# A two-group MoE encoder on one core: gate/up products of the next expert pair ahead of the down products of the current one

## The chip, the cores and the metric

The kernel runs on one core of a Trainium2 chip. The metric is the device time of one launch in microseconds (us). Everything is float32.

## What is computed

The reference is one step of a two-layer encoder over 576 tokens (512 of `x_prompt`, 64 of `x_sample`, width 1024). Layer 0 mixes tokens by banded attention, layer 1 by a convolution module; behind each comes the same kind of mixture of experts, which is what this change is about. Cut to that part:

```python
# N_GROUPS = 4, EXPERTS_PER_GROUP = 8, TOP_K_IN_GROUP = 2, D_MODEL = 1024, D_EXPERT = 256
g_w, g_idx = lax.top_k(g_probs, 1)               # one group per token
top_v, top_i = lax.top_k(in_group, TOP_K_IN_GROUP)   # two experts in it
...
hid = jax.nn.silu(jnp.einsum('nd,edf->nef', xt, w_gate[sl])) * jnp.einsum('nd,edf->nef', xt, w_up[sl])
hid = hid * gates[:, sl, None].astype(hid.dtype)
y = y + jnp.einsum('nef,efd->nd', hid, w_down[sl])
```

Each expert has 1 MB each of `w_gate`, `w_up` and `w_down`; a layer has 32 experts, 96 MB of weights.

## The kernel before

The kernel is written by hand for each engine: every engine runs a fixed list of instructions, and semaphores order them against each other. The stages follow one another: norm and attention, norm and router, experts of layer 0, gather and add; then norm and convolution, norm and router, experts of layer 1, gather and add; final norm.

**The expert stage.** The router gives each token two experts. Each expert has 64 slots (`CAP`), and two experts make a **pair** that fills 128 partitions; 16 pairs (`EPAIRS`) a layer. Tokens beyond 64 of one expert go to further (overflow) pairs, of which the data decide the number, at run time (`extra_turns`, `further`). For pair i (s = i % 2) the steps are:

- GpSimd gathers the pair's 128 rows of x from memory into `xe[s]` with one indirect DMA of 512 KB (L1095).
- *turn* (`ex_turn_pe`, L1168 to L1174): TensorE waits for these rows and transposes them in eight blocks into two PSUM banks (L1173). ScalarE copies one bank, VectorE the other, into `xte[s]` (`ex_turn_copy`, L1206).
- *gate/up* (`ex_up_pe`, L1176 to L1185): products of `xte[s]` with the pair's `w_gate` and `w_up` (L1183), into bank 2+s. ScalarE takes silu of one half into `sg` (L1211), VectorE multiplies it by the other half into `hid` (L1215).
- *down* (`ex_down_pe`, L1187 to L1202): TensorE transposes `hid` in two blocks (L1190), VectorE copies them into `hts` (L1219), TensorE waits for `w_down` and multiplies (L1200). ScalarE and VectorE each copy half of the result into `ysb[s]` (`ex_y_copy`, L1227).
- GpSimd scatters these 128 rows to memory with one indirect DMA of 512 KB (L1099).

`sg`, `hid` and `hts` exist once; `xe`, `xte`, `ysb` and the gate/up banks twice. Each engine runs its steps in the order in which `body` of `experts_pe`, `experts_act` and `experts_dve` names them, and a waiting instruction holds all that are behind it on its engine.

**Weights.** SyncE issues the loads (`experts_sync`). There are three buffers for gate/up (4 MB a pair, `GU_SLOTS`) and two for `w_down` (2 MB a pair). For pair i it waits until gate/up(i) is done, then issues the gate/up loads of pair i+3 (L1317), then waits until down(i) is done, and issues `w_down` of pair i+2 (L1321).

**GpSimd's list** (`experts_pool`): the gathers of pairs 0 and 1, some scatters for overflow rows, then for each i:

```python
if local + 2 < EPAIRS:
    pool.wait_ge(base.xt_mm, i + 1)      # turn(i) done
    rows_in(local + 2)                   # gather of pair i+2, L1095
...
pool.wait_ge(base.y_ev_a, i + 1 + FREE)  # both copies of y(i) done
pool.wait_ge(base.y_ev_d, i + 1 + FREE)
rows_out(local)                          # scatter of pair i, L1099
```

Behind the scatter of pair 14 it issues eight gathers (L1146) that bring finished result rows back to the tokens, then the scatter of pair 15, and, when that has landed and overflow pairs are done, the other gathers. The overflow pair, where there is one (here in layer 1), has its loads issued by SyncE when down(14) is done (L1366 to L1379).

Of the kernel before, what the change touches and what calls it, by code (L numbers as in the profile page):

```python
# [44 lines left out]
def encoder(nc, x_prompt, x_sample, cache_attn_k, cache_attn_v, cache_conv,  # L45
# [25 lines left out]
    EPAIRS = EXPERTS // 2  # L71
# [14 lines left out]
    with ExitStack() as ctx:  # L86
# [210 lines left out]
        base = ExpertSems("ex")  # L297
# [870 lines left out]
        def ex_turn_pe(pe, m, i, s, k):  # L1168
            pe.wait_ge(m.x_in[s], 16 * (k + 1))
            pe.wait_ge(m.xt_ev_a, i + FREE)  # L1170
            pe.wait_ge(m.xt_ev_d, i + FREE)
            for c in range(C):
                mm = nc.tensor.transpose(bank[c // 4][:, (c % 4) * P:(c % 4 + 1) * P], xe_pc[s][:, c, :], ident[:])  # L1173
            mm.then_inc(m.xt_mm, 1)  # L1174

        def ex_up_pe(pe, m, i, s, g, there):  # L1176
            pe.wait_ge(m.xt_ev_a, i + 1 + FREE)
            pe.wait_ge(m.xt_ev_d, i + 1 + FREE)
            pe.wait_ge(m.gu_in[g if m is base else 0], there)
            for c in range(C):  # L1180
                for e in range(2):
                    rr = slice(CAP * e, CAP * (e + 1))
                    mm = nc.tensor.matmul(bank[2 + s][rr, :], xte[s][:, c, rr], wgu[g][:, :, e, c, :],  # L1183
                                          start=c == 0, stop=c == C - 1)
            mm.then_inc(m.gu_mm, 1)  # L1185

        def ex_down_pe(pe, m, i, s, k, loads):  # L1187
            pe.wait_ge(m.hid, i + 1 + FREE)
            for c in range(FC):
                mm = nc.tensor.transpose(bank[4][:, c * P:(c + 1) * P], hid_pc[:, c, :], ident[:])  # L1190
            mm.then_inc(m.ht_mm, 1)
            pe.wait_ge(m.ht_ev, i + 1)
            pe.wait_ge(m.dn_in[s], 16 * loads * (k + 1))
            pe.wait_ge(m.y_ev_a, i + FREE)
            pe.wait_ge(m.y_ev_d, i + FREE)
            for h in range(2):
                for c in range(FC):
                    for e in range(2):
                        rr = slice(CAP * e, CAP * (e + 1))
                        mm = nc.tensor.matmul(bank[5 + h][rr, :], hts[:, c, rr], wdn[s][:, e, c, h * HALF:(h + 1) * HALF],  # L1200
                                              start=c == 0, stop=c == FC - 1)
            mm.then_inc(m.dn_mm, 1)  # L1202

        def ex_turn_copy(eng, copy, m, i, s, half, done):
            eng.wait_ge(m.xt_mm, i + 1)
            copy(xte[s][:, 4 * half:4 * half + 4, :], bank[half][:].rearrange("p (c r) -> p c r", c=4)).then_inc(done, 1)  # L1206

        def ex_silu_act(act, m, i, s):
            act.wait_ge(m.gu_mm, i + 1)
            act.wait_ge(m.hid, i + FREE)  # L1210
            nc.scalar.activation(sg, bank[2 + s][:, 0:FE], ACT.Silu).then_inc(m.silu, 1)  # L1211

        def ex_hid_dve(dve, m, i, s):
            dve.wait_ge(m.silu, i + 1)
            nc.vector.tensor_tensor(hid, sg, bank[2 + s][:, FE:2 * FE], ALU.mult).then_inc(m.hid, 1)  # L1215

        def ex_ht_dve(dve, m, i):
            dve.wait_ge(m.ht_mm, i + 1)
            nc.vector.tensor_copy(hts, bank[4][:, 0:FE].rearrange("p (c r) -> p c r", c=FC)).then_inc(m.ht_ev, 1)  # L1219

        def ex_y_copy(eng, copy, m, i, s, k, half, done):
            eng.wait_ge(m.dn_mm, i + 1)
            if m is base:
                eng.wait_ge(m.y_out[s], 16 * k + 16)
            else:
                eng.wait_ge(m.y_free, i + FREE)
            copy(ysb[s][:, half * HALF:(half + 1) * HALF], bank[5 + half][:]).then_inc(done, 1)  # L1227
# [4 lines left out]
        def gu_slot(l, local):  # L1232

            g = local % GU_SLOTS
            per_layer = len(range(g, EPAIRS, GU_SLOTS))
            return g, 32 * (per_layer * l + local // GU_SLOTS + 1)

        def turns(body, l):
            for local in range(EPAIRS):
                i = EPAIRS * l + local  # L1240
                body(i, i % 2, i // 2, local, local + 1 < EPAIRS)

        def extra_turns(eng, l, body):

            eng.wait_ge(further_known, 2 * l + 1)
            count = eng.value_load(over_count[0:1, 0:1], min_val=0, max_val=OPAIRS)
            with eng.If(count > 0):
                with eng.Fori(0, count) as it:
                    body(it)

        def experts_pe(pe, l):
            ex_turn_pe(pe, base, EPAIRS * l, 0, EPAIRS // 2 * l)

            def body(i, s, k, local, more):
                ex_up_pe(pe, base, i, s, *gu_slot(l, local))
                if more:
                    ex_turn_pe(pe, base, i + 1, (s + 1) % 2, k + (s + 1) // 2)
                ex_down_pe(pe, base, i, s, k, 1)

            turns(body, l)  # L1260

            extra = extras[l]

            def further(i):
                ex_turn_pe(pe, extra, i, 0, i)
                ex_up_pe(pe, extra, i, 0, GU_SLOTS - 1, 64 * (i + 1))
                ex_down_pe(pe, extra, i, 0, i, 2)

            extra_turns(pe, l, further)

        def experts_act(act, l):
            ex_turn_copy(act, nc.scalar.copy, base, EPAIRS * l, 0, 0, base.xt_ev_a)

            def body(i, s, k, local, more):
                ex_silu_act(act, base, i, s)
                if more:
                    ex_turn_copy(act, nc.scalar.copy, base, i + 1, (s + 1) % 2, 0, base.xt_ev_a)
                ex_y_copy(act, nc.scalar.copy, base, i, s, k, 0, base.y_ev_a)

            turns(body, l)  # L1280

            extra = extras[l]

            def further(i):
                ex_turn_copy(act, nc.scalar.copy, extra, i, 0, 0, extra.xt_ev_a)
                ex_silu_act(act, extra, i, 0)
                ex_y_copy(act, nc.scalar.copy, extra, i, 0, i, 0, extra.y_ev_a)

            extra_turns(act, l, further)

        def experts_dve(dve, l):
            ex_turn_copy(dve, nc.vector.tensor_copy, base, EPAIRS * l, 0, 1, base.xt_ev_d)

            def body(i, s, k, local, more):
                ex_hid_dve(dve, base, i, s)
                if more:
                    ex_turn_copy(dve, nc.vector.tensor_copy, base, i + 1, (s + 1) % 2, 1, base.xt_ev_d)
                ex_ht_dve(dve, base, i)
                ex_y_copy(dve, nc.vector.tensor_copy, base, i, s, k, 1, base.y_ev_d)

            turns(body, l)

            extra = extras[l]

            def further(i):
                ex_turn_copy(dve, nc.vector.tensor_copy, extra, i, 0, 1, extra.xt_ev_d)
                ex_hid_dve(dve, extra, i, 0)
                ex_ht_dve(dve, extra, i)
                ex_y_copy(dve, nc.vector.tensor_copy, extra, i, 0, i, 1, extra.y_ev_d)

            extra_turns(dve, l, further)
# [552 lines left out]
```

## Time and profile before

| | us |
|---|---|
| median of 3 runs (lowest, highest) | 1302.19 (1300.95, 1303.72) |
| the profiled execution, its own time | 1305.27 |
| its span in the trace | 1303.6 |
| TensorE busy in the span | 1067.0 (82%) |
| VectorE, ScalarE, GpSimd busy | 493.6, 289.5, 271.2 |
| granted TensorE clock, mean of the span | 0.91 |
| moved by DMA | 303.67 MB, mean 233 GB/s |

### The profile page before, as it was taken

Reading aid. Unit: us, or ns where it says so; the run is one execution under the profiler, and the core shown is the slowest. Engines: PE = TensorE matmul, PEld = TensorE weight load, DVE = VectorE, ACT = ScalarE, POOL = GpSimd, SP = SyncE. Lnnn points to the kernel's source line nnn. Section 1 sums busy time; section 2 is a strip of 40 time slices with the busy share of each in tenths; the row PEclk is TensorE's granted clock in tenths of the full one; section 3 lists DMA queues with packets and bytes.
Section 4 is the critical chain, followed back from the end, with each engine's and each line's share of the span. In section 5 each row is a group of like instructions: output and inputs, shape, how many; then the busy total and the mean of one; then the engine's idle time right before and its main releaser. Section 6 shows DMA issues by size and latency. Waiting matters only on the chain.

```text
span 1303.6 us, 14394 instructions
## 1 busy us (share of the span) xinstructions
PE 1067.0 (82%) x5242; PEld 617.5 (47%) x5242; DVE 493.6 (38%) x1066; ACT 289.5 (22%) x616; POOL 271.2 (21%) x289
## 2 busy tenths in 40 slices
PE   6999999996995897777762999987985987778780
PEld 5777777773453333333321777653543333333320
DVE  3234444443247111101116499994455111111116
ACT  3223232222111110000003355544111100000002
POOL 2000000000001221111033288860003110011033
PEclk9999999996996899888885899998995998888995
DMA  8953333212506899999955932100027999999764
GB/s 278 388 159 105 107 107 106 79 55 105 233 24 236 318 419 420 420 421 420 407 191 132 338 102 64 32 19 6 33 92 282 417 421 421 420 420 420 319 236 144
DMA packets 107791, 303.67 MB, mean 233 GB/s; under 512 B 18248, under 2 KB 65480, under 8 KB 82745
## 3 DMA queue, kind: packets, MB, share of 16 engines
q1 hardware_dynamic: 85481, 254.74, 50.5%
q0 software_dynamic: 22256, 48.22, 10.2%
q8 instruction: 33, 0.54, 0.2%
q14 instruction: 21, 0.17, 0.0%
HBM read 278.34 MB, written 57.12 MB: 257 GB/s over the span
## 4 chain that ended last, share of the span: by engine, by line
PE 66%; issue 16%; DVE 12%; ACT 2%; DMA 2%; POOL 1%; DVEq 0%; SPq 0%; another core or an unknown queue 0%; POOLq 0%
PE bank L1183 17%; PE bank L1200 11%; PE bank L522 10%; PE bank L421 8%; PE bank L549 4%; PE bank L1173 3%; DVE bank L1646 2%; PE bank L572 2%; PE bank L588 2%; PE bank L613 2%; PE bank L346 1%; PE bank L938 1%; DVE work L1219 1%; POOL ring L1146 1%; DVE work L1206 1%
## 5 line engine op out<-in xcount | busy, mean ns | idle before, releaser
L1200 PE MATMUL bank<-ring,work 128*64 128x512 f32 x528 | 149.9, 720 | 89.9 <-issue 80.4
L1183 PE MATMUL bank<-ring,work 128*64 128x512 f32 x704 | 158.9, 604 | 4.7 <-issue 3.8
L522 PE MATMUL bank<-arena,ring 128*128 128x288 f32 x512 | 131.9, 412 | 0.0
L1462 PE MATMUL bank<-arena,work 128*128 128x288 f32 x512 | 127.4, 410 | 5.1 <-DVE work L1627 2.6
L1200 PEld LDWEIGHTS bank<-ring,work 128*64 128x64 f32 x528 | 46.8, 165 | 170.1 <-issue 159.3
L421 PE MATMUL bank<-ring,arena 128*128 128x512 f32 x256 | 116.6, 611 | 7.4 <-ACT arena L1577 6.6
L1593 POOL TENSOR_TENSOR ring<-ring 128x606 f32<-128x606 f32 x76 | 103.8, 1366 | 57.0 <-ACT ring L1542 47.3
L1462 PEld LDWEIGHTS bank<-arena,work 128*128 128x128 f32 x512 | 97.6, 192 | 34.5 <-issue 4.0
L522 PEld LDWEIGHTS bank<-arena,ring 128*128 128x128 f32 x512 | 94.9, 190 | 32.6 <-issue 7.9
L1183 PEld LDWEIGHTS bank<-ring,work 128*64 128x64 f32 x704 | 56.2, 140 | 103.0 <-issue 101.7
L1215 DVE TENSOR_TENSOR work<-work,bank 128x256 f32<-128x256 f32 x33 | 13.9, 421 | 226.2 <-ACT work L1211 226.2
L1646 DVE SCALAR_TENSOR_TENSOR bank<-work,ring,bank 128x606 f32<-128x606 f32 x129 | 98.9, 846 | 0.0
L1183 PE MATMUL bank<-arena,work 128*64 128x512 f32 x352 | 79.3, 603 | 2.5 <-DVE work L1206 2.5
L1095 POOL DMA_INDIRECT work<-x_rows,tok_at x32 | 33.1, 1034 | 228.2 <-DVEq L1035 219.0
L421 PEld LDWEIGHTS bank<-ring,arena 128*128 128x128 f32 x256 | 49.0, 196 | 64.7 <-issue 63.2
L1542 ACT ACTIVATE ring<-work,ring 128x606 f32<-128x606 f32 x84 | 65.5, 797 | 37.1 <-POOL ring L1593 37.1
L346 PE MATMUL bank<-ident,arena 128*128 128x128 f32 (+1 forms) x160 | 28.1, 335 | 47.2 <-DVE arena L332 47.2
L1099 POOL DMA_INDIRECT y_sorted<-work,slot_at x16 | 15.8, 988 | 239.8 <-DVE work L1227 239.8
L1227 DVE COPY work<-bank 128x512 f32<-128x512 f32 x17 | 11.8, 692 | 134.7 <-PE bank L1200 134.7
L712 ACT ACTIVATE work<-work,soft 64x192 f32<-64x192 f32 (+4 forms) x80 | 42.6, 533 | 86.5 <-DVE soft L798 86.5
L1211 ACT ACTIVATE work<-bank 128x256 f32<-128x256 f32 x33 | 12.7, 385 | 214.8 <-PE bank L1183 208.5
L900 POOL DMA_DIRECT2D out<-work x8 | 4.6, 575 | 250.3 <-ACT work L705 250.3
(252 smaller groups left out, 1297.8 us busy)
## 6 DMA issues: line engine op xcount, KB each, us to landing
ring<-in_w_down SPq DMA_DIRECT2D x32, 2048.0 KB, 27.9
ring<-in_w_gate SPq DMA_DIRECT2D x22, 2048.0 KB, 22.3
ring<-in_w_up SPq DMA_DIRECT2D x22, 2048.0 KB, 30.7
arena<-in_w_gate SPq DMA_DIRECT2D x10, 2048.0 KB, 20.7
arena<-in_w_up SPq DMA_DIRECT2D x10, 2048.0 KB, 31.0
ring<-in_w_qkv SPq DMA_DIRECT2D x24, 512.0 KB, 6.0
y_sorted<-gain POOLq DMA_DIRECT2D x8, 1536.0 KB, 5.7
work<-in_w_pw SPq DMA_DIRECT2D x16, 512.0 KB, 5.0
```

The costliest lines, as they stand in the source:

```text
L346: mm = nc.tensor.transpose(b[:, (c % 4) * P:(c % 4) * P + r], src[0:r, j, c, :], ident[0:r, 0:r])
L421: mm = nc.tensor.matmul(bank[3 + h][0:rows[j], :], act_t[:, c, j * P:j * P + rows[j]], w[:, c, h * HALF:(h + 1) * HALF], start=c == 0, sto ...
L522: mm = nc.tensor.matmul(bank[b][:, 0:HT], wa[s][:, w, c, :], xt[:, c, h * HT:(h + 1) * HT], start=c == 0, stop=c == C - 1)
L549: mm = nc.tensor.matmul(bank[0][:, j * P:(j + 1) * P], xt_tile(c, j), wa[s][:, 2, c, :], start=c == 0, stop=c == C - 1)
L712: ins = nc.scalar.activation(prob[0:q, b, h, 0:nk], prob[0:q, b, h, 0:nk], ACT.Exp, bias=soft[0:q, b, 0, h:h + 1], accum_out=soft[0:q, b, ...
L1173: mm = nc.tensor.transpose(bank[c // 4][:, (c % 4) * P:(c % 4 + 1) * P], xe_pc[s][:, c, :], ident[:])
L1183: mm = nc.tensor.matmul(bank[2 + s][rr, :], xte[s][:, c, rr], wgu[g][:, :, e, c, :], start=c == 0, stop=c == C - 1)
L1200: mm = nc.tensor.matmul(bank[5 + h][rr, :], hts[:, c, rr], wdn[s][:, e, c, h * HALF:(h + 1) * HALF], start=c == 0, stop=c == FC - 1)
L1462: mm = nc.tensor.matmul(bank[2 * h + w][:, 0:GT], wp[s][:, w, c, :], xt[:, c, h * GT:(h + 1) * GT], start=c == 0, stop=c == C - 1)
L1542: nc.scalar.activation(out, u[s][:, m:m + OUTS], ACT.Copy, scale=cvec[s][:, m:m + 1]).then_inc(prod_done, 1)
L1593: pool.tensor_tensor(side[s], side[s], prod[turn(s, m)], ALU.add).then_inc(side_done, 1)
L1646: steps.behind(V.scalar_tensor_tensor(a, src(t), w(t), a, ALU.mult, ALU.add))
```

## The change

The order of the steps in the three `body` functions changes. Before, an iteration is gate/up(i), turn(i+1), down(i). After, it is gate/up(i+1), turn(i+2), down(i), with gate/up(0) and turn(1) put ahead of the first iteration's. ScalarE and VectorE are reordered to match. The overflow pairs, GpSimd's list and SyncE's list are as before.

```diff
@@ experts_pe
             def body(i, s, k, local, more):
-                ex_up_pe(pe, base, i, s, *gu_slot(l, local))
+                if local == 0:
+                    ex_up_pe(pe, base, i, s, *gu_slot(l, local))
+                    ex_turn_pe(pe, base, i + 1, 1 - s, k)
                 if more:
-                    ex_turn_pe(pe, base, i + 1, (s + 1) % 2, k + (s + 1) // 2)
+                    ex_up_pe(pe, base, i + 1, 1 - s, *gu_slot(l, local + 1))
+                if local + 2 < EPAIRS:
+                    ex_turn_pe(pe, base, i + 2, s, k + 1)
                 ex_down_pe(pe, base, i, s, k, 1)
@@ experts_act
             def body(i, s, k, local, more):
-                ex_silu_act(act, base, i, s)
+                if local == 0:
+                    ex_silu_act(act, base, i, s)
+                    ex_turn_copy(act, nc.scalar.copy, base, i + 1, 1 - s, 0, base.xt_ev_a)
                 if more:
-                    ex_turn_copy(act, nc.scalar.copy, base, i + 1, (s + 1) % 2, 0, base.xt_ev_a)
+                    ex_silu_act(act, base, i + 1, 1 - s)
+                if local + 2 < EPAIRS:
+                    ex_turn_copy(act, nc.scalar.copy, base, i + 2, s, 0, base.xt_ev_a)
                 ex_y_copy(act, nc.scalar.copy, base, i, s, k, 0, base.y_ev_a)
@@ experts_dve
             def body(i, s, k, local, more):
-                ex_hid_dve(dve, base, i, s)
+                if local == 0:
+                    ex_hid_dve(dve, base, i, s)
+                    ex_turn_copy(dve, nc.vector.tensor_copy, base, i + 1, 1 - s, 1, base.xt_ev_d)
+                if local + 2 < EPAIRS:
+                    ex_turn_copy(dve, nc.vector.tensor_copy, base, i + 2, s, 1, base.xt_ev_d)
+                ex_ht_dve(dve, base, i)
                 if more:
-                    ex_turn_copy(dve, nc.vector.tensor_copy, base, i + 1, (s + 1) % 2, 1, base.xt_ev_d)
-                ex_ht_dve(dve, base, i)
+                    ex_hid_dve(dve, base, i + 1, 1 - s)
                 ex_y_copy(dve, nc.vector.tensor_copy, base, i, s, k, 1, base.y_ev_d)
```

## Rows read from the trace of the kernel before

**Rows 1.** Page, part 2: the span in 40 slices of 32.6 us.
```profile
PEclk9999999996996899888885899998995998888995
DMA  8953333212506899999955932100027999999764
GB/s 278 388 159 105 107 107 106 79 55 105 233 24 236 318 419 420 420 421 420 407 191 132 338 102 64 32 19 6 33 92 282 417 421 421 420 420 420 319 236 144
```

**Rows 2.** Busy time by stretches, expert stage of layer 0.
```profile
core 0: us, PE busy (x) PEld busy (x) DVE busy (x) ACT busy (x) POOL busy (x), PEclk, DMA share, GB/s
436.00:487.00 51.00, 47.96 (x235) 18.65 (x234) 8.64 (x17) 6.22 (x12) 10.90 (x11) 1.00 1.01 413
487.00:662.00 175.00, 131.66 (x589) 55.43 (x589) 22.47 (x43) 16.17 (x31) 19.19 (x19) 0.90 0.98 405
```

**Rows 3.** Timeline (start, duration, engine, line, operation [idle before]): TensorE and VectorE, layer 0.
```profile
435.25 1.16 PE L1173 MATMUL bank<-ident,work 128*128 128x128 f32 x8
437.52 3.65 PE L1200 MATMUL bank<-ring,work 128*64 128x512 f32 x16 [0.77 <-DVE work L1219]
441.01 7.04 PE L1183 MATMUL bank<-ring,work 128*64 128x512 f32 x32
441.22 0.69 DVE L1227 COPY work<-bank 128x512 f32<-128x512 f32 x1 [3.75 <-PE bank L1200]
447.97 1.16 PE L1173 MATMUL bank<-ident,work 128*128 128x128 f32 x8
448.98 0.50 PE L1190 MATMUL bank<-ident,work 128*128 128x128 f32 x2
449.17 0.69 DVE L1206 COPY work<-bank 128x512 f32<-128x512 f32 x1 [0.24 <-PE bank L1173]
450.25 3.65 PE L1200 MATMUL bank<-ring,work 128*64 128x512 f32 x16 [0.76 <-DVE work L1219]
460.70 1.16 PE L1173 MATMUL bank<-ident,work 128*128 128x128 f32 x8
```

**Rows 4.** Timeline of GpSimd and of SyncE's issues, layer 0.
```profile
435.35 0.37 SPq L1317 DMA_DIRECT2D ring<-in_w_gate  x1
441.22 0.37 SPq L1321 DMA_DIRECT2D ring<-in_w_down  x1
442.77 0.98 POOL L1099 DMA_INDIRECT y_sorted<-work,slot_at  x1 [12.16 <-DVE work L1227]
444.06 1.02 POOL L1095 DMA_INDIRECT work<-x_rows,tok_at  x1 [0.30 <-issue]
448.08 0.37 SPq L1317 DMA_DIRECT2D ring<-in_w_gate  x1
```

**Rows 5.** Issue to landing: first gather and turn; line L1099 by itself (last row).
```profile
416.15 1.11 POOL L1095 DMA_INDIRECT work<-x_rows,tok_at  x1 [100.82 <-DVEq L1035]
420.23 1.97 PE L1173 MATMUL bank<-ident,work 128*128 128x128 f32 x8 [5.99 <-DMA work<-x_rows,tok_at]
...
DMA to landing us min/median/max: 3.7/8.5/9.7
```

**Rows 6.** Timeline of TensorE: down products that waited, layer 0.
```profile
491.29 5.35 PE L1200 MATMUL bank<-ring,work 128*64 128x512 f32 x16 [3.64 <-issue]
559.06 5.90 PE L1200 MATMUL bank<-ring,work 128*64 128x512 f32 x16 [6.24 <-issue]
627.95 5.59 PE L1200 MATMUL bank<-ring,work 128*64 128x512 f32 x16 [6.48 <-issue]
660.79 6.23 PE L1200 MATMUL bank<-ring,work 128*64 128x512 f32 x16 [5.20 <-issue]
675.84 3.65 PE L1200 MATMUL bank<-ring,work 128*64 128x512 f32 x16 [0.52 <-DVE work L1219]
```

**Rows 7.** End of layer 0's expert stage: GpSimd's issues, and the chain's last scatter.
```profile
668.61 0.97 POOL L1099 DMA_INDIRECT y_sorted<-work,slot_at  x1 [18.74 <-DVE work L1227]
679.02 0.96 POOL L1146 DMA_INDIRECT ring<-y_sorted,early_slot  x1 [0.30 <-issue]
681.56 3.73 DMA y_sorted<-gain,slot_at
```

**Rows 8.** Timeline of TensorE and SyncE's issue, layer 1: first pair, pair 14, overflow pair.
```profile
1000.89 8.58 PE L1183 MATMUL bank<-ring,work 128*64 128x512 f32 x32 [0.91 <-ACT work L1206]
1009.40 1.16 PE L1173 MATMUL bank<-ident,work 128*128 128x128 f32 x8
1233.71 6.49 PE L1200 MATMUL bank<-ring,work 128*64 128x512 f32 x16 [4.24 <-issue]
1241.88 0.36 SPq L1377 DMA_DIRECT2D arena<-in_w_gate  x1
1256.26 8.78 PE L1183 MATMUL bank<-arena,work 128*64 128x512 f32 x32 [2.50 <-DVE work L1206]
```

## The prediction

> **What bounds the kernel now.** I read the page first, then the stretches of the expert stage, then the instructions of each engine in order of time, and last the landing times. The two long plateaus near 420 GB/s on the page are the expert stages of the two layers [rows 1]. In the stretch of layer 0 from 487 to 662 us the DMA engines are busy 0.98 of the time, TensorE 131.7 of 175 us [rows 2]: weights pace this part. The stretch before it (436 to 487 us) is paced by TensorE (48.0 of 51 us): it consumes what was loaded ahead, one pair each 12.72 us (437.52 to 450.25, [rows 3]). After that, TensorE waits some 2 to 6 us ahead of each down product, for its `w_down` (no engine is named, "issue") [rows 6]. Down products run from 437.52 to 675.84 us: 15 pairs of 15.9 us.
>
> The thing to see for this change is a second loop that is now hidden. For pair i+2, the rows of x come by an indirect gather that GpSimd issues (L1095). GpSimd's order is a list: gather(i+2), then scatter(i) of the result rows (L1099), then gather(i+3). Scatter(i) waits for the copies of y(i). So gather(i+3) starts 1.3 us behind scatter(i): 444.06 against 442.77 for i=0 [rows 4]. Before, TensorE turns pair 3 at 460.70 us [rows 3], 16.6 us after that gather was issued, and never waits for it.
>
> **The change, step by step.** The arithmetic, the tiles, the bytes and the GpSimd and SyncE lists stay. Only the order on TensorE, ScalarE and VectorE changes.
>
> *Order on TensorE.* Before: gate/up(i), turn(i+1), down(i). After: gate/up(i+1), turn(i+2), down(i). What the old order made the weights wait for is now better covered: gate/up(i+1) can run while `w_down(i)` lands. But look at turn(i+2). Its gather is issued after scatter(i-1), that is after down(i-1). Between down(i-1) and turn(i+2) there was gate/up(i), turn(i+1), down(i) and gate/up(i+1); now there is only gate/up(i+1), 6.96 us (441.01 to 447.97, [rows 3]). And down(i) is queued behind the waiting turn(i+2). The loop closes: down(i-1), copy of y, scatter, gather, turn(i+2), down(i).
>
> *Length of that loop, from rows.* The end of down(0) is 437.52+3.65 = 441.17; gather(3) is issued at 444.06 [rows 3, 4]: 2.9 us, for y copy (0.69), GpSimd's wake-up and one scatter issue. Then the gather's time to landing, G. Then turn to the two small transposes 1.01 (447.97 to 448.98), these to the down product 1.27 (448.98 to 450.25), the down product 3.65 [rows 3]. Sum: 2.9 + 1.01 + 1.27 + 3.65 = 8.8 us, plus G. ScalarE and VectorE are in the same order as TensorE, so their copies add nothing beyond the 1.27: gate/up(i+1) is 7 us old when turn(i+2) runs, and silu and product of pair i are done.
>
> *G, from both sides.* With no loads running, gather(0) was issued at 416.15 and TensorE began at 420.23: 4.1 us, the lower end [rows 5]. The upper end is what the old schedule allows, 16.6 us. Nearest is the scatter: the same 512 KB, the same queue, the same issuer: 3.7 us at the least, 8.5 at the median and 9.7 at most [rows 5]; the 3.7 is the one issued at 681.56, behind the last loads [rows 7]; the median is one of those among the loads. The gather is issued 1.3 us behind a scatter that still has 8.5-1.3 = 7.2 us to go, and its own 512 KB at half of 420 GB/s take 2.5: 9.7; with a full idle latency behind it, 7.2+3.7 = 10.9. I take 10.5, and 8.4 to 10.9 for the range (7.2 plus 1.2 at full rate is the low one). Will the loads still run beside it? Yes: SyncE issues `w_down`(i+2) when down(i) is done and gate/up(i+4) right behind it (its wait, gate/up(i+1), is past by then), so 6 MB, 15 us at 420 GB/s, start with each scatter. Before, they were issued apart, 441.22 and 448.08 for i=0 and i=1 [rows 4].
>
> The Trainium skill ("DMA: Bandwidth & Descriptors", "Anatomy of one DMA — SWDGE (gpsimd) path") fits one DMA of this path as 2.0 us + bytes/436e3; for 512 KB that is an estimate of 3.2 us. The idle scatter (3.7) agrees, the scatters among loads (8.5) do not. By the page the turn would never wait, and the time would be that of the rival "quick gather" below; I follow the rows.
>
> *TensorE's clock.* The new wait is 2.9 + 10.5 - 6.96 = 6.4 us in each pair. Now, behind waits of 3.6 to 6.5 us, the down product takes 5.4 to 6.2 us instead of 3.65 and the granted clock averages 0.90 over the stretch, so part of each such product runs at the lower level, 1.2 GHz [rows 2, 6]. After the new wait comes the turn; the one at 420.23 behind idle time took 1.97 instead of 1.16 [rows 3, 5]. I add 1.9 us per pair (0.8 for the turn, the rest for small transposes and the start of down), range 1.4 to 2.8: the excess on down products is 1.7 to 2.8 in these rows [rows 6, 8], and some of the wait may not cost any.
>
> *Period:* 8.8 + 10.5 + 1.9 = 21.2 us per pair. This is above the pace of the weights, about 17.2 us (560 to 628 us: the down products at 559.06 and 627.95 are four pairs apart, [rows 6]), so the DMA engines will have idle time and the gather loop rules.
>
> *Layer 0.* The first pairs: turn(1) begins at 435.25; gate/up(1) now waits for its copies (1.9 us, turn start to the end of VectorE's copy, 447.97 to 449.86) and starts at 437.3; then 6.96 + 1.01 + 1.27 + 3.65: down(0) ends at 450.1, 9 us later than now. Rows of pair 2 were gathered at the very start, so no wait there. Turns 3 to 15 are in the loop: 13 x 21.2 = 275.6, to 725.7. Pair 14's down follows gate/up(15) alone: 6.96+1.27+3.65 = 11.9, so it ends at 737.6; now at 660.79+6.23 = 667.0: **+70.6**. Behind that, GpSimd issues scatter(14), eight gathers of results and scatter(15) (668.61 to 681.56, [rows 7]). Down(15) is now much closer to down(14), so only GpSimd's own list counts: 681.56 becomes 680.3 on the old axis, -1.3. Layer 0: +69.3.
>
> *Layer 1* begins the same way: gate/up(0) at 1000.89, turn(1) at 1009.40, so down(0) ends at 1024.3, down(14) at 1024.3+275.6+11.9 = 1311.8; now 1233.71+6.49 = 1240.2 [rows 8]: **+71.6**. Here one overflow pair follows. Its weights are requested when down(14) is done. Now TensorE starts its gate/up at 1256.26, 16.1 us after, held up by gate/up(15) and down(15) in between. After, only down(15) is left (4.9 us) and 3.6 us of turn and copies: 8.5 us, and its weights, issued 1.7 us after down(14) [rows 8], may not have landed. Gain between 1 and 7.5 us; I take 4. Layer 1: +67.6.
>
> *Sum:* +137 us. The profiled execution took 1305.3 (span 1303.6), 3.1 over the median of the runs, 1302.2. Against the median: **1439 us**.
>
> What the change saves, the wait for `w_down`, was up to 6 us a pair; it is gone, but only since the loads are no longer what is late.
>
> **Rivals.** (That the change doesn't do what it says is none: the order is written out, instruction by instruction.)
> 1. *Quick gather, faster.* If G falls below 6.96-2.9 = 4.0 us, no turn waits. Weights pace the stage as now, and the end is better: gate/up(15) is done before `w_down(14)` lands (660.8, [rows 6]), so down(14) ends at 664.5 instead of 667.0 and GpSimd's list starts 2.5 earlier (and saves the 1.3); in layer 1 2.8 and 4. Together -10.6: 1292 us. For it: the idle 3.7 and 4.1 us. Against it: the scatter's median of 8.5, DMA engines at 0.98 of the time. The point is G = 4.0.
> 2. *Quick gather, but the first loads late.* As rival 1, but `w_down(2)` and gate/up(4) are issued at 450.1 instead of 441.2 and 448.1, and the queue runs dry for an estimated 4 us in each layer (gate/up(3), issued at 435.35 [rows 4], is 4 MB, 10 us, done near 446 with nothing behind it): the weights pace everything, so 8 us come back, and gate/up(15) itself starts behind a wait at the low clock (+2 each). -10.6+8+4 = +1.4: 1304 us, no change.
> 3. *Half-way.* G of 5 to 8 us, since the loads of one pair are issued with the scatter and have not filled the rings by then. At 6.5 the period is 8.8+6.5+1.5 = 16.8, under the weights' 17.2, so these pace it again, and with the late first loads of rival 2 it is some 1310; for 8 us it is 18.5 and 26 x 2.7 = 70 us less than forecast: 1310 to 1369.
> 4. *Slower still.* G stays at 10.9 or more and the clock takes 2.8: 22.5 a pair, +34: 1473. If the loads in one bundle push G to 12, 1500.
>
> **How the numbers follow.** Forecast with its bounds (1385 to 1475) 0.8; rival 3 0.09; rival 4 beyond 1475 0.04; rival 1 0.04; rival 2 0.03. The range of the forecast, 8.4 to 10.9 for G and 1.4 to 2.8 for the clock, is 18.6 to 22.5 us a pair, 26 pairs: 1371 to 1473; I cut it at 1385, as both low ends together are unlikely, and close at 1475. The forecast has one sign with rivals 3 and 4, so slower is 0.93. About 0.2% (2.6 us) is what can be told from no change: faster 0.05, same 0.02.
>
> **What the new profile would show.** Right: TensorE waits ahead of the turn (L1173), 5 to 8 us, for the x rows, thirteen times a layer; gather issues about 21 us apart; down products at an even distance; no wait left ahead of L1200 but the 0.8 us for the transposes; DMA share down to about 0.8 and under 350 GB/s in the stage; scatter landings still at 8 to 9 us. Wrong: pairs 17 us apart with the wait ahead of gate/up (L1183) and 420 GB/s (rivals 1 to 3); or a scatter median near 4 us. If the period is right but not G, the wait ahead of the turn tells by how much; if that wait is 6.4 us and the period still differs, the clock term was mis-sized.

## The result, and the profile after

| | before | after |
|---|---|---|
| median of 4 runs | 1301.6 us | 1486.3 us |
| profiled execution, own time | 1305.3 us | 1484.9 us |
| its span | 1303.6 us | 1483.2 us |

The ratio is 1.1405, with a 95% interval of 1.1387 to 1.1424: 185 us slower. The forecast was 1439 us, the range 1385 to 1475. The direction and the place were right, the size was too small, and the time lies 11 us above the range.

The page of the kernel after, parts 2 and 4 (the chain that ended last, by line), against [rows 1]:

```profile
PE   6999999979866667566653999879867567576771
PEclk9999999969978687686775999999968687777896
DMA  9933333142367786876655922000277776867673
GB/s 288 342 100 108 115 104 109 49 186 118 121 261 287 285 331 262 331 282 278 262 173 134 339 59 57 1 21 29 99 315 296 308 316 270 332 274 295 257 268 127
...
DMA work<-x_rows,tok_at 19%; PE bank L1200 12%; PE bank L522 9%; PE bank L421 7%; PE bank L1173 4%; PE bank L1183 4%; PE bank L549 3%; DVE bank L1658 2%; PE bank L572 2%; PE bank L588 2%; PE bank L613 2%; POOL y_sorted L1099 2%; PE bank L346 1%; PE bank L938 1%; POOL ring L1146 1%
```

The plateaus at 420 GB/s are gone, and the first name on the chain is a DMA: the gather of x rows. The stretch of layer 0 that stands in [rows 2] reads, after (busy time by stretches):

```profile
487.00:662.00 175.00, 119.32 (x456) 45.68 (x456) 16.32 (x32) 12.04 (x23) 17.04 (x17) 0.74 0.73 291
```

The DMA share fell from 0.98 to 0.73 and the granted clock from 0.90 to 0.74; TensorE is less busy too. Neither loads nor arithmetic pace the stage now. One turn of the loop in the timeline of the kernel after, TensorE, SyncE's issues and GpSimd (start, duration, engine, line, operation [idle before]):

```profile
489.35 6.35 PE L1200 MATMUL bank<-ring,work 128*64 128x512 f32 x16 [0.69 <-DVE work L1219]
495.53 7.03 PE L1183 MATMUL bank<-ring,work 128*64 128x512 f32 x32
495.74 0.37 SPq L1333 DMA_DIRECT2D ring<-in_w_down  x1
496.15 0.47 SPq L1329 DMA_DIRECT2D ring<-in_w_gate  x1
497.30 0.99 POOL L1099 DMA_INDIRECT y_sorted<-work,slot_at  x1 [19.59 <-DVE work L1227]
498.59 1.02 POOL L1095 DMA_INDIRECT work<-x_rows,tok_at  x1 [0.31 <-issue]
509.88 1.97 PE L1173 MATMUL bank<-ident,work 128*128 128x128 f32 x8 [7.32 <-DMA work<-x_rows,tok_at]
511.64 0.64 PE L1190 MATMUL bank<-ident,work 128*128 128x128 f32 x2
512.96 6.49 PE L1200 MATMUL bank<-ring,work 128*64 128x512 f32 x16 [0.69 <-DVE work L1219]
```

Down ends at 495.70; the scatter goes out at 497.30, the gather at 498.59; 11.3 us later the turn starts, and down behind it. Against [rows 3] the down product takes 6.4 instead of 3.65 and the turn 1.97 instead of 1.16. Time from issue to landing of the gathers (L1095) and of the scatters (L1099), after, in this order:

```profile
DMA to landing us min/median/max: 3.9/10.9/11.8
...
DMA to landing us min/median/max: 4.0/8.5/10.5
```

The scatters land as late as in [rows 5] (8.5). The gathers' landing, for which the trace before had no row, is 10.9 us. The period is the distance of turn 3 from turn 15, over 12; layer 0, then layer 1:

```profile
463.90 1.97 PE L1173 MATMUL bank<-ident,work 128*128 128x128 f32 x8 [7.31 <-DMA work<-x_rows,tok_at]
738.24 1.97 PE L1173 MATMUL bank<-ident,work 128*128 128x128 f32 x8 [3.59 <-DMA work<-x_rows,tok_at]
...
1133.03 1.97 PE L1173 MATMUL bank<-ident,work 128*128 128x128 f32 x8 [6.97 <-DMA work<-x_rows,tok_at]
1404.39 1.16 PE L1173 MATMUL bank<-ident,work 128*128 128x128 f32 x8 [3.11 <-DMA work<-x_rows,tok_at]
```

That is 274.34/12 = 22.86 us in layer 0 and 271.36/12 = 22.61 us in layer 1.

### The profile page after: what moved, and what is told of

Its sections match the earlier page's. It is cut to its first block, busy times and chain, and to the rows that moved or that the text cites. A ratio compares the mean times of both kernels' runs of the same rounds, so it can differ in the third digit from the quotient of the medians.

```text
span 1483.2 us, 14394 instructions
## 1 busy us (share of the span) xinstructions
PE 1123.7 (76%) x5242; PEld 630.3 (42%) x5242; DVE 490.5 (33%) x1066; ACT 289.3 (20%) x616; POOL 271.8 (18%) x289
## 4 chain that ended last, share of the span: by engine, by line
PE 50%; DMA 21%; issue 12%; DVE 11%; POOL 3%; ACT 2%; SPq 0%; POOLq 0%; DVEq 0%
DMA work<-x_rows,tok_at 19%; PE bank L1200 12%; PE bank L522 9%; PE bank L421 7%; PE bank L1173 4%; PE bank L1183 4%; PE bank L549 3%; DVE bank L1658 2%; PE bank L572 2%; PE bank L588 2%; PE bank L613 2%; POOL y_sorted L1099 2%; PE bank L346 1%; PE bank L938 1%; POOL ring L1146 1%
## 5 line engine op out<-in xcount | busy, mean ns | idle before, releaser
L1173 PE MATMUL bank<-ident,work 128*128 128x128 f32 x264 | 60.2, 401 | 193.5 <-DMA work<-x_rows,tok_at 193.5
L1200 PE MATMUL bank<-ring,work 128*64 128x512 f32 x528 | 180.1, 845 | 22.9 <-DVE work L1219 22.9
L1183 PE MATMUL bank<-ring,work 128*64 128x512 f32 x704 | 158.7, 604 | 6.0 <-issue 3.4
L1206 DVE COPY work<-bank 128x512 f32<-128x512 f32 x33 | 22.8, 691 | 407.0 <-PE bank L1173 406.7
L1173 PEld LDWEIGHTS bank<-ident,work 128*128 128x128 f32 x264 | 48.2, 215 | 220.7 <-DMA work<-x_rows,tok_at 216.6
L522 PEld LDWEIGHTS bank<-arena,ring 128*128 128x128 f32 x512 | 94.9, 190 | 32.6 <-issue 7.9
L1095 POOL DMA_INDIRECT work<-x_rows,tok_at x32 | 33.0, 1031 | 228.7 <-DVEq L1035 219.5
L1099 POOL DMA_INDIRECT y_sorted<-work,slot_at x16 | 15.8, 986 | 307.2 <-DVE work L1227 307.2
L1099 POOL DMA_INDIRECT y_sorted<-gain,slot_at x16 | 15.9, 994 | 279.1 <-DVE gain L1227 278.5
L1206 ACT COPY work<-bank 128x512 f32<-128x512 f32 x33 | 19.3, 584 | 222.9 <-PE bank L1173 222.9
## 6 DMA issues: line engine op xcount, KB each, us to landing
ring<-in_w_up SPq DMA_DIRECT2D x22, 2048.0 KB, 18.9
```

The lines of the kernel that those rows point to most:

```text
L522: mm = nc.tensor.matmul(bank[b][:, 0:HT], wa[s][:, w, c, :], xt[:, c, h * HT:(h + 1) * HT], start=c == 0, stop=c == C - 1)
L1099: pool.indirect_dma_start(y_sorted, bass.IndirectOffsetOnAxis(slot_at[:, local:local + 1], 0), ysb[local % 2], None, bounds_check=EXPERTS ...
```

## Experiments

The theory to test: down(i-1), y copy, scatter, gather, turn(i+2), down(i) form a loop, whose length sets the period. The rivals: the new order costs time by itself; the weights, now requested in one bundle, do it; the gather is late for a reason other than the loads. Each kernel was run beside the kernel before on the same chip, and each ratio is to that.

### 1. The gather issued ahead of the wait for y

```diff
+                if local == 0:
+                    pool.wait_ge(base.xt_mm, i + 1)
+                    rows_in(2)
-                if local + 2 < EPAIRS:
-                    pool.wait_ge(base.xt_mm, i + 1)
-                    rows_in(local + 2)
+                if local + 3 < EPAIRS:
+                    pool.wait_ge(base.xt_mm, i + 2)
+                    rows_in(local + 3)
```

> The kernel after the change, with GpSimd's list changed in one point: gather(i+3) is issued when turn(i+1) is done, ahead of the wait for the copies of y(i) and of scatter(i). Theory (the loop down(i-1), y copy, scatter, gather, turn(i+2), down(i) is what costs 185 us): the gather then has some 19 us of TensorE work ahead of its turn against the 11 us it needs, the wait ahead of the turn goes, and the weights pace the stage again: 1292 to 1310 us, likeliest 1302. Rival (the reordered engines themselves, or the weights issued in one bundle, cost the time): it stays above 1400 us.

Measured: 1310.3 us against 1305.1, ratio 1.0042 (1.0028 to 1.0056). Of 185 us, 180 are gone with an edit of one DMA's place. No turn but the first of a stage waits for a gather; the waits stand ahead of gate/up now and name weights. TensorE's timeline in this kernel, and its stretch 436 to 487 us:

```profile
488.86 7.09 PE L1186 MATMUL bank<-arena,work 128*64 128x512 f32 x32 [0.89 <-DMA arena<-in_w_up]
505.65 8.47 PE L1186 MATMUL bank<-ring,work 128*64 128x512 f32 x32 [3.85 <-DMA ring<-in_w_up]
...
436.00:487.00 51.00, 46.65 (x231) 18.49 (x232) 8.15 (x16) 6.22 (x12) 10.94 (x11) 1.00 0.94 378
```

So the new order itself and the bundled requests cost some 5 us, not 185. The DMA share of 0.94 against 1.01 in [rows 2] is 3.6 us of 51 in which the DMA engines ran dry: the late first loads of the prediction's rival 2.

### 2. The same gather place in the kernel before

> The kernel before, with the same earlier gather. TensorE never waited for a gather there, so the theory expects no change: 1302 us, within 3. If earlier gathers help by themselves (less contention, a better place among the loads), it gets faster by more than 5 us, and then the first experiment would owe part of its gain to that.

Measured: 1302.6 us, ratio 0.9980 (0.9967 to 0.9993). The time is the expected one, but the ratio is clear of 1: the earlier gather is worth some 2.6 us by itself. So of the 180 us that experiment 1 won back all but these are the loop, and what the new order costs in experiment 1 is nearer to 8 us than to 5.

### 3. Gather ahead of the scatter, both still behind y

```diff
-                if local + 2 < EPAIRS:
+                if local == 0:
                     pool.wait_ge(base.xt_mm, i + 1)
-                    rows_in(local + 2)
+                    rows_in(2)
...
                 pool.wait_ge(base.y_ev_d, i + 1 + FREE)
+                if local + 3 < EPAIRS:
+                    pool.wait_ge(base.xt_mm, i + 2)
+                    rows_in(local + 3)
                 rows_out(local)
```

> The kernel after the change, with gather(i+3) issued ahead of scatter(i), but both still behind the copies of y(i). Tells what of the gather's 11 us is due to the scatter ahead of it. Theory (the two share the queue): the gather is issued 1.3 us earlier and lands 8.5 us after its issue instead of 10.9, so a period is 3.7 us shorter, 26 periods, -96: 1390 us, a little less if the shorter wait also saves clock. Rival (the landing time is the loads' doing alone): only the 1.3 us go, -34: 1452 us.

Measured: 1378.3 us, ratio 1.0563 (1.0521 to 1.0604). Timeline of GpSimd and TensorE, and the scatters' landing times:

```profile
523.31 1.03 POOL L1095 DMA_INDIRECT work<-x_rows,tok_at  x1 [16.77 <-ACT work L1230]
524.64 1.00 POOL L1099 DMA_INDIRECT y_sorted<-work,slot_at  x1 [0.30 <-issue]
531.42 1.97 PE L1176 MATMUL bank<-ident,work 128*128 128x128 f32 x8 [2.85 <-DMA work<-x_rows,tok_at]
...
DMA to landing us min/median/max: 4.9/11.0/11.9
```

The roles are exchanged: the gather is there 8.1 us after its issue in this turn and 8.7 on average in layer 0 (issue to start of the turn, turns 3 to 15), and the scatter, now second, takes 11.0 at the median. The period (down(1) at 460.75, down(13) at 687.87) is 18.9 us, 3.9 less than after, where 3.7 was expected; the time is 12 us under the expected 1390. The rival's 1452 is excluded.

### 4. The turn behind down

```diff
-                if local + 2 < EPAIRS:
-                    ex_turn_pe(pe, base, i + 2, s, k + 1)
                 ex_down_pe(pe, base, i, s, k, 1)
+                if local + 2 < EPAIRS:
+                    ex_turn_pe(pe, base, i + 2, s, k + 1)
```

with the copies on ScalarE and VectorE moved in the same way.

> The kernel after the change, with turn(i+2) moved behind down(i) on TensorE, ScalarE and VectorE; GpSimd's list as it is. Theory: down(i) no longer stands behind the turn that waits for a gather, and between down(i) and turn(i+3) lie turn, its copies, gate/up, small transposes and down, 1.0+1.9+7.0+1.3+3.7 = 14.9 us against 2.9+11 = 13.9 needed: no wait for gathers or a small one, the weights pace the stage at 17.2 us a pair, 1300 to 1320 us. Rival (the wait only moves to another place): over 1400 us.

Measured: 1312.6 us, ratio 1.0060 (1.0043 to 1.0077). What TensorE waited for, over the span (total us, times, longest):

```profile
PE bank L1183 <- DMA ring<-in_w_up: 34.1, 12, 4.6
PE bank L1183 <- DMA arena<-in_w_up: 20.2, 6, 6.5
...
PE bank L1173 <- DMA work<-x_rows,tok_at: 17.4, 8, 8.7
```

The gather waits are 17.4 us in eight, against 193.5 in 28 after; the first turns of the two layers, which wait in the kernel before too, are 14.7 of either sum. GpSimd's list is untouched here: it is enough that down(i) doesn't stand behind the turn.

### 5. TensorE kept busy in the wait

```diff
+                    if local > 0:
+                        for _ in range(52):
+                            nc.tensor.transpose(bank[7][:, 0:P], ident[:], ident[:])
                     ex_turn_pe(pe, base, i + 2, s, k + 1)
```

> The kernel after the change, with 52 transposes of the identity into an unused PSUM bank put ahead of each turn that waits (some 6.6 us of TensorE work in a wait of 7.2 us), so that TensorE is not idle there. Tells what the low clock costs behind the wait. Theory: turn back from 1.97 to 1.16, down from 5.96 on average to 3.65, so the period falls from 22.9 to about 19.7 us, 26 periods, -82: 1404 us; the wait for the gather itself stays. Rival (turn and down are slow for another reason, as the loads beside them): no change, 1486 us.

Measured: 1431.2 us, ratio 1.1000 (1.0980 to 1.1019), so some 53 us less than after by the ratios, where 82 were expected. The profiled execution, from which the rows are, is the fastest of the five (1421.5), 63 us under that of after. TensorE's timeline, and the stretch 487 to 662 us:

```profile
506.69 5.31 PE L1200 MATMUL bank<-ring,work 128*64 128x512 f32 x16 [0.88 <-DVE work L1219]
511.83 7.03 PE L1183 MATMUL bank<-arena,work 128*64 128x512 f32 x32
518.79 5.90 PE L1263 MATMUL bank<-ident 128*128 128x128 f32 x52
526.50 1.16 PE L1173 MATMUL bank<-ident,work 128*128 128x128 f32 x8 [1.81 <-DMA work<-x_rows,tok_at]
527.50 0.40 PE L1190 MATMUL bank<-ident,work 128*128 128x128 f32 x2
528.77 3.65 PE L1200 MATMUL bank<-ring,work 128*64 128x512 f32 x16 [0.88 <-DVE work L1219]
...
487.00:662.00 175.00, 155.91 (x948) 87.41 (x945) 17.02 (x33) 13.40 (x26) 19.07 (x19) 0.99 0.84 336
```

The granted clock is 0.99 instead of 0.74. The same loads run beside it, at 336 GB/s instead of 291, and still turn and down take 1.16 and 3.65. So it is the clock, not contention, that made them slow. The period fell from 22.86 to 20.09 (down(1) at 467.23, down(13) at 708.27); it didn't fall by the whole 3.2, as one down product of layer 0 (506.69) was slow still and the gathers took 11.1 us instead of 10.9 (issue to start of the turn, means of turns 4 to 15). In layer 1 three down products were slow (5.35, 5.97 and 6.58 us), and the period fell by 2.1 only, from 22.61 to 20.5. And 20 us remain although the clock is nearly full: the loop without its clock term.

### 6. An eighth of the expert weights

```diff
+            part = C * FE if p < GU_SLOTS else C * FE // 8
...
-                sp.dma_start(wgu[s][:, w, :, :, :].rearrange("p e c f -> p e (c f)"),
+                sp.dma_start(wgu[s][:, w, :, :, :].rearrange("p e c f -> p e (c f)")[:, :, 0:part],
```

and the same for `w_down`. The kernel leaves out seven eighths of these weights and multiplies by stale ones in their place, so only its times count.

> The kernel after the change, with only an eighth of the expert weights loaded (for gate/up from pair 3 on, for down from pair 2 on, in both layers), so the experts' products use stale weights; all waits and instructions stay. Theory (the gather lands late since it shares the DMA engines with the weights): a gather lands 4 to 5.5 us after its issue, the wait ahead of the turn falls to 0 to 1.5 us, no clock is lost, period 12.7 to 14.2 us instead of 22.9: 1225 to 1265 us. Rival (11 us is what a gather behind a scatter takes on GpSimd's queue anyway): the wait stays at 7 us and the time above 1450 us.

Measured: 1230.1 us, in a single execution; the period of layer 0 is 13.4 us. Gathers' and scatters' landing times, and a turn:

```profile
DMA to landing us min/median/max: 3.6/4.5/7.0
...
DMA to landing us min/median/max: 2.7/4.2/5.3
...
496.17 1.16 PE L1173 MATMUL bank<-ident,work 128*128 128x128 f32 x8 [1.43 <-DMA work<-x_rows,tok_at]
```

With the same order, list and number of DMAs the gather lands in 4.5 us instead of 10.9, and the waits shrink to 0.7 us on average in layer 0 (10 of 13 turns). So the 10.9 us are the loads' doing, together with the scatter ahead (experiment 3). The Trainium skill has a rule that fits ("DMA: Bandwidth & Descriptors", "Queues, rings and completion order"): each DMA engine serves the queues in turn, a packet at a time. No run here shows in what order packets were served.

### 7. A hybrid that takes the new order where weights pace

Experiment 1 with the old order for pairs 0 to 3:

```diff
-                if local == 0:
+                if local <= 4:
                     ex_up_pe(pe, base, i, s, *gu_slot(l, local))
...
-                if more:
+                if local >= 4 and more:
                     ex_up_pe(pe, base, i + 1, 1 - s, *gu_slot(l, local + 1))
```

> The first experiment's kernel (gather ahead of the wait for y), with the old order of TensorE, ScalarE and VectorE for pairs 0 to 3 and the new one from pair 4 on. Theory (what is left of the first experiment's loss is that the first w_down and gate/up loads are requested 9 us late while nothing else is queued): SyncE's requests come as early as before the change, the DMA share from 436 to 487 us is back at 1.0, and some 3 to 4 us a layer come back: 1302 us, range 1298 to 1306, next to 1305 before and 1310 for the first experiment. Rival (the loss is all in the end of the stage): 1310 us.

Measured: 1302.2 us, ratio 1.0000 (0.9989 to 1.0011). The DMA share of 436 to 487 us is 1.02 again, and the 5 us are back. Yet no gain is left, though TensorE is done earlier. TensorE and GpSimd at the end of layer 0, and TensorE at the overflow pair of layer 1:

```profile
667.77 3.65 PE L1203 MATMUL bank<-ring,work 128*64 128x512 f32 x16 [0.69 <-DVE work L1222]
679.92 1.03 POOL L1099 DMA_INDIRECT y_sorted<-gain,slot_at  x1 [0.30 <-issue]
686.26 1.02 POOL L1149 DMA_INDIRECT ring<-y_sorted,late_slot  x1 [5.31 <-SPq L1425]
...
1251.91 9.23 PE L1186 MATMUL bank<-arena,work 128*64 128x512 f32 x32 [6.49 <-DMA arena<-in_w_up]
```

Down(15) starts at 667.77 against 675.84 in [rows 6], 8 us earlier. But scatter(15) stands behind eight gathers in GpSimd's list (679.92 against 681.56 in [rows 7]), lands later behind their rows, and the late gathers start at 686.26, where they did before (686.63). In layer 1 the overflow pair waits 6.5 us for its weights.

### 8. The early gathers behind scatter(15)

```diff
-                if local == EARLY_PAIRS:
+                if local == EPAIRS - 1:
```

> As the hybrid, with GpSimd's eight early gathers of result rows moved behind scatter(15). Theory: down(15) now ends 5 us after down(14), so scatter(15) stood ready behind eight gathers' issues and landed late behind their rows; issued first it lands while they are issued, and the gathers that wait for it start 2 us earlier in layer 0, nothing in layer 1 where the overflow pair ends last: 2 us faster than the hybrid, 1300 us. Rival: the same as the hybrid, as GpSimd issues the same number of DMAs either way.

Measured: 1303.8 us, ratio 1.0015 (1.0003 to 1.0026): a miss. It isn't faster than the hybrid, and the two intervals overlap, so it isn't shown to be slower either. GpSimd's timeline:

```profile
672.10 0.98 POOL L1099 DMA_INDIRECT y_sorted<-gain,slot_at  x1 [3.80 <-DVE gain L1230]
690.44 0.99 POOL L1149 DMA_INDIRECT ring<-y_sorted,late_slot  x1 [3.53 <-DMA ring<-y_sorted,early_slot]
695.39 0.99 POOL L1149 DMA_INDIRECT ring<-y_sorted,late_slot  x1 [2.67 <-DMA ring<-y_sorted,early_slot]
```

Scatter(15) went out 8 us earlier, but each late gather waits for the landing of the early one of its tile, and these were now late; in the profiled executions layer 1's first gate/up starts 2.9 us later than in the hybrid (1003.58 against 1000.71). I had counted issues, not landings.

### 9 to 11. The two ends of the stage

Two edits on the hybrid: the overflow pair's gate/up loads wait for gate/up(14) instead of down(14), and in the second kernel also the eight early gathers move ahead of scatter(14). The third has the earlier x gathers and both edits under the old order of the engines.

```diff
-            sp.wait_ge(base.dn_mm, EPAIRS * (l + 1) - 1)
+            sp.wait_ge(base.gu_mm, EPAIRS * (l + 1) - 1)
             with sp.If(count > 0):
...
+                    sp.wait_ge(base.dn_mm, EPAIRS * (l + 1) - 1)
                     sp.dma_start(wdn[0][:, e, :, :].rearrange("p c n -> p (c n)"),
...
-                if local == EARLY_PAIRS:
+                if local == EARLY_PAIRS - 1:
```

> The hybrid, with the overflow pair's gate/up loads requested when gate/up(14) is done instead of down(14) (its w_down still waits for down(14)). In the hybrid TensorE reaches the overflow pair at 1244 us and then waits 6.5 us for these loads. Theory (the 8 us that the new order gains at the end of TensorE's list are lost to what follows): that wait goes and with it the low clock behind it, 4 to 8 us, layer 1 only: 1296 us, against 1302 for the hybrid. Rival (the loads then compete with w_down(14) and (15), or GpSimd's list is what ends last): 1302 us.

> As the kernel above, with GpSimd's eight early gathers of result rows moved ahead of scatter(14) (behind scatter(13), whose landing they wait for anyway). Theory: in layer 0 GpSimd's list ends the stage: scatter(15) waits behind these eight issues, 10.4 us; ahead of scatter(14) they are issued while TensorE computes down(14), and scatter(15) goes out 3 to 4 us earlier: 1292 us. Rival (they are then issued too late, as scatter(13) lands 8.5 us after its issue, and now hold up scatter(14)): 1296 us or more.

> The kernel before with the earlier gather of x rows and both edits of the end (overflow loads, place of the early gathers), its order of TensorE, ScalarE and VectorE untouched. Theory: there TensorE's own list ends last (gate/up(15) and down(15) behind down(14)), so neither edit is worth anything: 1302 us, within 3. Rival (these edits alone make the gain of the two kernels above): 1292 to 1297 us.

Measured against 1305.4 us before: 1298.9 us, ratio 0.9952 (0.9936 to 0.9967); 1298.1 us, ratio 0.9936 (0.9916 to 0.9956); 1301.3 us, ratio 0.9969 (0.9955 to 0.9984). The first two are faster than both kernels of this study. TensorE at the overflow pair in the first of them; GpSimd in layer 0 in the second; TensorE at the overflow pair in the third:

```profile
1246.65 7.09 PE L1186 MATMUL bank<-arena,work 128*64 128x512 f32 x32 [0.97 <-DVE work L1209]
1256.73 0.70 PE L1193 MATMUL bank<-ident,work 128*128 128x128 f32 x2 [3.00 <-DVE work L1218]
1258.14 6.23 PE L1203 MATMUL bank<-ring,work 128*64 128x512 f32 x16 [0.71 <-DVE work L1222]
```

```profile
676.73 1.00 POOL L1099 DMA_INDIRECT y_sorted<-gain,slot_at  x1 [0.30 <-issue]
683.78 1.02 POOL L1149 DMA_INDIRECT ring<-y_sorted,late_slot  x1 [6.05 <-SPq L1426]
```

```profile
1254.43 7.09 PE L1186 MATMUL bank<-arena,work 128*64 128x512 f32 x32 [0.97 <-DVE work L1209]
```

The overflow pair's gate/up starts 5.3 us earlier than in the hybrid. But its small transposes now wait 3.0 us for VectorE's product, and the down product behind them runs slow (6.23), so that it ends 2.7 us earlier (1264.37 against 1267.04). VectorE waits there for ScalarE's silu, which starts 2.1 us behind the end of gate/up; what holds it the trace doesn't tell. The early gathers of the second kernel bring scatter(15) forward by 3 us as expected. But layer 1's first gate/up starts only 0.4 us earlier than in the first kernel (1000.39 against 1000.80), and its overflow pair waits 4.6 us for its weights again: the expected 1292 was missed, and the two kernels can't be told apart.

The third kernel came out within 3 us of my 1302, but not for my reason, that neither edit is worth anything there. The overflow edit is: from the end of down(15) to the end of the overflow pair's down product it takes 15.0 us, against 18.2 in experiment 2's kernel, which has the same early x gathers and neither edit. The other 1.5 us are lost ahead of it, as layer 1 starts later (1002.03 against 1000.52). Together, 0.9969 can't be told from experiment 2's 0.9980.

How much of the 0.5% is due to the new order stays open. With both edits the new order has 0.9936 and the old one 0.9969, some 4 us, and the intervals just touch. The kernel that would settle it was not run: the old order with the early x gathers and the overflow edit alone. From the profiled spans, an estimate for it is 1300.3 - 3.2 = 1297.1 us, and the first kernel above has 1297.3. By this estimate the new order is worth nothing here, though TensorE is done 8 us earlier in each layer.

## Why the prediction was right or wrong

**The mechanism was right.** The loop is there, with the waits ahead of L1173 and the even period, thirteen times a layer, and it goes when either of its links is cut (experiments 1 and 4). Scatters still take 8.5 us, loads lost their plateau, TensorE waits 6.9 us on average ahead of the turn in layer 0 (forecast 6.4).

**The step that failed is the clock term.** The prediction put 1.9 us a pair on what the low clock costs behind the new wait, with 2.8 as the upper bound; it cost 3.2. By terms of the period, in layer 0 after:

| term | forecast | measured |
|---|---|---|
| down's end to the gather's issue | 2.9 | 2.9 |
| gather, issue to the start of the turn (G) | 10.5 | 10.9 |
| turn, transposes, down at full clock | 5.9 | 5.9 |
| clock: turn + transposes + down | 1.9 | 0.75 + 0.05 + 2.36 = 3.2 |
| period | 21.2 | 22.86 |

The mean down product between these turns takes 6.01 us (3.65 at full clock); turn to transposes is 1.76 (1.01). I had both prices at hand, 1.7 to 2.8 for a down product behind a wait and 0.8 for a turn, and put the second inside the first, as if the turn used up part of the slow time. It didn't: the turn ran wholly at the lower level (granted clock 0.50 from 509.9 to 511.6 us), down began there (0.50 from 513 to 518 us), and lost 2.4 us on average, as much as down products had lost directly behind a wait (1.7 to 2.8). The prediction had named the sign of this: a wait near 6.4 us with another period. The range repeated the error, since 2.8 was the bound of one product, not of the sum: 26 times the 0.36 us beyond it are 9 of the 11 us by which the range was missed. Experiment 5 shows that this term is the clock: with TensorE busy in the wait, turn and down are back at 1.16 and 3.65 us in 11 of the 12 periods of layer 0.

**The sum.** Down(14) of layer 0 ended 92.4 us later than before (759.45 against 667.02), where 70.6 was forecast; from layer 1's first gate/up (1095.56 against 1000.89) to its down(14) (1423.22 against 1240.20) it took 88.4 us more, where 71.6 was forecast. These are 21.8 and 16.8 us too few, by the periods above; another 3.5 were lost between the layers and 0.6 at the overflow pair. 137 and these 43 are 180, the difference of the profiled executions (179.6). The medians differ by 5 us more, as the profiled execution before was 3.7 us above its median and the one after 1.4 below; I had taken the sum over to the median as it stood.

**G** was 0.4 us too small, 10 us of the sum. Its mean of 10.9 is the forecast's upper bound, and without the last gather of the layer (issued at 730.67, 7.6 us) the mean is 11.2, beyond it. The way to it, one DMA of the same size plus its share behind the other, was right, and experiment 3 shows both parts of it (8.7 first, 11.0 second). The 3.2 us estimated from the fit of the Trainium skill ("DMA: Bandwidth & Descriptors", "Anatomy of one DMA — SWDGE (gpsimd) path") lie below the 4.5 of experiment 6 and far from all the loaded ones.

**The ends.** Down(14) of layer 0 to scatter(15) shrank by 1.3 us, as forecast; missed was that scatter(15) lands 2 us later behind eight gathers (5.8 us after its issue instead of 3.7). The overflow pair gained 3.8 us up to its gate/up (12.3 us behind down(14) instead of 16.1; forecast 4), and waited 6.4 us for its weights.

**Rivals.** Rivals 1 and 2 had the right price for another kernel: with the gather out of the way (experiment 1) the result is 5 us slower than before, near rival 2's no change and far from rival 1's -10.6. The early loads were late as described there, and the gain at the end didn't arrive, since GpSimd's list ends the stage.

## What to carry to other kernels

When a step is moved ahead on one engine, go through the lists of the engines that feed it: a gather that was never waited for can have all its slack from work that now comes later, and a DMA issued behind a store closes a loop through the product that the store came from. Issue a load when its buffer is free, not behind a store that waits for results. Price a wait of several us on TensorE as the wait plus the low clock on all that follows it, each product by its own slow duration.

## What the hardware showed that I had not expected

Two indirect DMAs of 512 KB issued 1.3 us apart beside a full stream of loads take 8.5 to 8.7 us for the first and 10.9 to 11.0 for the second, whichever is the gather; with an eighth of the loads the scatter takes 4.2 and the gather behind it 4.5. Behind a wait of some 7 us TensorE stayed at 1.2 GHz (granted clock 0.50) through a turn and two transposes (3.1 us) and still for the larger part of the down product behind them (6.01 instead of 3.65 us on average).
